# A two-block transformer kernel on one Trainium2 core: a new order of the steps where one stage hands x to the next

## The reference

```python
for l in range(2):
    h = rms_norm(x, g[0]); x = x + 0.5 * rms_norm(swiglu(h, w1[l,0], w3[l,0], w2[l,0]), g[1])
    h = rms_norm(x, g[2]); x = x + rms_norm(mixer_block(h, w_in[l], ...), g[3])
    h = rms_norm(x, g[4]); x = x + rms_norm(cross_attention(h, rms_norm(mem), ...), g[5])
    h = rms_norm(x, g[6]); x = x + 0.5 * rms_norm(swiglu(h, w1[l,1], w3[l,1], w2[l,1]), g[7])
```

## Time and profile before

| | us |
|---|---|
| runs of the kernel before: lowest, median, highest | 2435.52, 2442.23, 2451.49 |
| the profiled execution, whole | 2452.16 |
| its span, from first to last instruction | 2450.3 |
| TensorE busy in the span | 2280.1 |
| VectorE busy | 1712.3 |
| ScalarE busy | 1182.3 |
| mean granted TensorE clock, share of full speed | 0.956 |

### The profile page before, as it was taken

One profiled execution on the slowest core, in us unless ns is written; L12 is line 12 of the kernel. 1 busy time (PEld: TensorE's weight loads), 2 busy tenths in 40 slices (PEclk: granted clock), 3 DMA queues, 4 the chain that ended last, 5 costly groups with the idle time before them and its releaser, 6 DMA issues.

```text
span 2450.3 us, 43494 instructions
## 1 busy us (share of the span) xinstructions
PE 2280.1 (93%) x17809; PEld 2178.7 (89%) x17809; DVE 1712.3 (70%) x2733; ACT 1182.3 (48%) x1843; POOL 91.6 (4%) x86
## 2 busy tenths in 40 slices
PE   6998898999999999989898998999899989797998
PEld 5977798999999897889797998999897889797998
DVE  6666887986665797777555665665797787555664
ACT  2564446764544434455434454444434454534443
POOL 1000000110110000000000110010000000000010
PEclk7998999999999999899999999999899899899999
DMA  8634585667657463346443765666553345453664
GB/s 238 194 106 144 161 257 156 201 190 225 190 177 222 138 181 91 108 142 194 128 157 114 203 185 162 184 195 194 161 178 94 104 146 182 128 173 96 198 184 134
DMA packets 399909, 405.08 MB, mean 165 GB/s; under 512 B 18182, under 2 KB 392312, under 8 KB 399713
## 3 DMA queue, kind: packets, MB, share of 16 engines
q1 hardware_dynamic: 396177, 389.27, 52.5%
q0 software_dynamic: 3536, 13.04, 1.7%
HBM read 401.17 MB, written 1.09 MB: 164 GB/s over the span
## 4 chain that ended last, share of the span: by engine, by line
PE 72%; DVE 18%; ACT 6%; issue 4%; DMA 1%; DVEq 0%; ACTq 0%; POOL 0%; POOLq 0%
PE gemm_ps L934 46%; PE gemm_ps L937 15%; DVE weights_lo L1557 6%; DVE x_res L2023 4%; PE misc_ps L1075 2%; PE misc_ps L1076 2%; ACT weights_hi L1191 1%; DVE mod_partial L1656 1%; ACT e L1358 1%; PE misc_ps L872 1%; PE misc_ps L1108 1%; ACT squares L1315 1%; PE misc_ps L1093 1%; PE misc_ps L1072 1%; DVE y L1731 1%
## 5 line engine op out<-in xcount | busy, mean ns | idle before, releaser
L1557 DVE TENSOR_TENSOR weights_lo<-raw_weights,weights_hi 128x1024 fp32r<-128x1024 f32 x704 | 836.8, 1199 | 430.4 <-ACT weights_hi L1191 426.9
L1191 ACT CAST weights_hi<-raw_weights 128x1024 fp32r<-128x1024 f32 x704 | 717.6, 1032 | 658.9 <-PE gemm_ps L934 457.1
L934 PE MATMUL gemm_ps<-h_hi,weights_hi 128*128 128x256 f32 x3280 | 939.0, 286 | 20.0 <-DVE h_lo L1685 8.7
L934 PE MATMUL gemm_ps<-h_lo,weights_hi 128*128 128x256 f32 x3280 | 922.1, 281 | 0.0
L934 PE MATMUL gemm_ps<-h_hi,weights_lo 128*128 128x256 f32 x3280 | 921.5, 281 | 0.0
L934 PEld LDWEIGHTS gemm_ps<-h_hi,weights_hi 128*128 128x128 f32 x3280 | 631.5, 193 | 27.7 <-issue 21.0
L934 PEld LDWEIGHTS gemm_ps<-h_lo,weights_hi 128*128 128x128 f32 x3280 | 630.9, 192 | 3.4 <-issue 3.0
L934 PEld LDWEIGHTS gemm_ps<-h_hi,weights_lo 128*128 128x128 f32 x3280 | 630.1, 192 | 0.0
L2023 DVE SCALAR_TENSOR_TENSOR x_res<-zp,param_cols,x_res 128x256 f32<-128x256 f32 x480 | 196.7, 478 | 0.0
L937 PE MATMUL gemm_ps<-weights_hi,hidh 128*128 128x256 f32 x688 | 189.9, 276 | 0.0
L937 PE MATMUL gemm_ps<-weights_hi,hidl 128*128 128x256 f32 x688 | 189.9, 276 | 0.0
(11 more groups left out here) (324 smaller groups left out, 3144.9 us busy)
## 6 DMA issues: line engine op xcount, KB each, us to landing
raw_weights<-in_ffn_w_dram SPq DMA_DIRECT2D x256, 512.0 KB, 4.2
raw_weights<-in_w_in_dram SPq DMA_DIRECT2D x200, 512.0 KB, 3.8
raw_weights<-in_w_mod_dram SPq DMA_DIRECT2D x48, 512.0 KB, 5.0
raw_weights<-in_w_up_dram SPq DMA_DIRECT2D x44, 512.0 KB, 4.6
raw_weights<-in_xattn_kv_dram SPq DMA_DIRECT2D x32, 512.0 KB, 3.7
raw_weights<-in_w_out_dram SPq DMA_DIRECT2D x24, 512.0 KB, 4.1
raw_weights<-in_w_down_dram SPq DMA_DIRECT2D x20, 512.0 KB, 4.7
raw_weights<-in_w_branch_dram SPq DMA_DIRECT2D x16, 512.0 KB, 4.6
```

What stands on the lines that cost most here:

```text
L934: mm = pe.matmul(ps[:, c, 0:T], w[:, m, kt, c * P:(c + 1) * P], x[:, f, :], start=start, stop=stop_)
L1191: act.copy(unit_of(WH, m % SPLIT, u), unit_of(RAWB, u["raw"] % RAW, u)).then_inc(sems["weights_rounded"], 1)
L1557: dve.tensor_tensor(unit_of(WL, m % SPLIT, u), unit_of(RAWB, u["raw"] % RAW, u), unit_of(WH, m % SPLIT, u), ALU.subtract).then_inc(sems["w ...
```

## The change

All of it is at the seven changes of stage.

1. **Late conversion.** For the last unit m of a stage's last product (c = 3; `w2` and `xattn_o`, not `w_out_2`), `hi(m+3)` is issued behind `y_rstd`'s two instructions on ScalarE, and `lo(m+3)` on VectorE just ahead of `row_wide`, which stands behind all updates and splits. The seven changes have three of `w2`, two of `xattn_o` and two of `w_out_2`.
2. **Ten matmuls** (`warm`) on the constant tiles ones and ident, fp32, 128x128 by 128x128, into PSUM bank 2, behind the stage's last work on TensorE and ahead of the first turn. Nothing reads what they write.
3. **Turning.** Tiles 0 to 3 are all turned ahead of the first unit, into four banks (f % 4); a turn waits for the split of tile f-4. Tiles 4 and 5 are turned ahead of k-tiles 2 and 3 of the first unit, 6 and 7 ahead of k-tiles 0 and 1 of the second. The order on VectorE stays.
4. **The row.** VectorE's wide copy becomes a step of its own (`row_wide`) inside `enter`, ahead of `lo(m+4)` and `lo(m+5)` in VectorE's queue. The step `x_row` (TensorE's two matmuls, ScalarE's copy) goes behind the first unit of the second gemm.

```diff
     def gemm(...):
             u["turn_h"] = turns_of_h.pop(j, None)
+            u["late"] = j == n - 1 and k.get("c") == 3 and w != "w_out_2"
             units.append(u)
             readers[x[0]] = u["n"]
             add("unit", **u)
+            S.extend(row_next)
+            row_next.clear()
         S.extend(held)
         held.clear()
+        row_next.extend(row_due)
+        row_due.clear()
         add(evac, **p)
...
     def enter(key, name, at_):
+        s = new_stat()
         k = dict(key=key, v=xv[0])
         h = dict(buf="H", gen=key, src="turned", ...)
+        add("warm", n=10)
         add("update_x", p=0, **res)
-        for f in (0, 1):
-            add("turn_h", f=f, **k)
+        add("update_x", p=1, **res)
+        for f in range(4):
+            add("turn_h", f=f, s=s if f == 3 else None, **k)
         for p in range(4):
-            if p == 0:
-                add("update_x", p=1, **res)
-            elif p > 1:
+            if p > 1:
                 add("update_x", p=p, **res)
             for f in (2 * p, 2 * p + 1):
                 add("split", f=f, **h)
-        for j in range(2):
-            turns_of_h[j] = [dict(k, f=f) if f < NF else None for f in range(4 * j + 2, 4 * j + 6)]
-        s = new_stat()
+        turns_of_h[0] = [None, None, dict(k, f=4), dict(k, f=5)]
+        turns_of_h[1] = [dict(k, f=6), dict(k, f=7), None, None]
         add("x_rstd_tok", key=key, v=xv[0])
-        held.append(("x_row", dict(key=key, s=s)))
+        add("row_wide", key=key)
+        row_due.append(("x_row", dict(key=key, s=s)))
...
         def pe_turned(k):
-            if f >= 3:
-                pe.wait_ge(sems["vec_split"], at("split", "H", k["key"], f - 3))
+            if f >= 4:
+                pe.wait_ge(sems["vec_split"], at("split", "H", k["key"], f - 4))
+        def pe_warm(k):
+            ...
+            for i in range(k["n"]):
+                pe.matmul(TURN[:, 0:P], ONES[:], IDENT[:], start=True, stop=True)
         def pe_turn_h(k):
+            if k["f"] == 3:
+                stat_free(k["s"])
...
     # ScalarE's walk of the list
             if kind == "unit":
-                hi(k["m"] + AHEAD)
+                if k["late"]:
+                    state["late"] = k["m"] + AHEAD
+                else:
+                    hi(k["m"] + AHEAD)
             if kind in parts:
                 parts[kind](k)
+            if kind == "y_rstd" and state["late"] is not None:
+                hi(state["late"])
+                state["late"] = None
...
     # VectorE's walk of the list
+            if kind == "row_wide" and state["late"] is not None:
+                lo(state["late"])
+                state["late"] = None
             if kind == "unit":
-                lo(k["m"] + AHEAD)
+                if k["late"]:
+                    state["late"] = k["m"] + AHEAD
+                else:
+                    lo(k["m"] + AHEAD)
```

More of the change, by code:

```diff
@@ L96, in plan @@
     turns_of_h = {}
+    row_due, row_next = [], []
     def add(kind, **k):
@@ L755, in source @@
         if k["src"] == "turned":
-            return PB[:, k["f"] % 3, 0:T]
+            return PB[:, k["f"] % 4, 0:T]
         return BUF[k["src"]][:, k["f"], :]
@@ L868, in pe_turned @@
             pe.wait_ge(sems["vec_norm"], at("x", k["v"], f // 2))
-            if f >= 3:
-                pe.wait_ge(sems["vec_split"], at("split", "H", k["key"], f - 3))
+            if f >= 4:
+                pe.wait_ge(sems["vec_split"], at("split", "H", k["key"], f - 4))
             for t in range(TT):
-                mm = pe.transpose(PB[:, f % 3, t * P:(t + 1) * P], XT[:, t, f * P:(f + 1) * P], IDENT[:])
+                mm = pe.transpose(PB[:, f % 4, t * P:(t + 1) * P], XT[:, t, f * P:(f + 1) * P], IDENT[:])
             mm.then_inc(sems["pe_norm"], 1)
             up("pe_norm", ("h_turned", k["key"], f))
+        def pe_warm(k):
+            if state["att"] is not None:
+                pe.wait_ge(sems["vec_attn"], at("o_raw", *state["att"]))
+                if state["att"][0][:4] == "diff":
+                    pe.wait_ge(sems["act_attn"], at("o_sq", *state["att"]))
+            for i in range(k["n"]):
+                pe.matmul(TURN[:, 0:P], ONES[:], IDENT[:], start=True, stop=True)
         def pe_turn_h(k):
@@ L1170, in pe_mem_turn @@
                 up("pe_norm", ("mem_ps", k["l"], half))
-        parts = dict(unit=pe_unit, window=pe_window, params=pe_params, turn_x=pe_turn_x, mod=pe_mod, mod_col=pe_mod_col, bias=pe_bias, stat=pe_stat, x_stat=pe_x_stat, turn_h=pe_turn_h, x_tok=pe_x_tok, x_row=pe_x_row,
+        parts = dict(unit=pe_unit, warm=pe_warm, window=pe_window, params=pe_params, turn_x=pe_turn_x, mod=pe_mod, mod_col=pe_mod_col, bias=pe_bias, stat=pe_stat, x_stat=pe_x_stat, turn_h=pe_turn_h, x_tok=pe_x_tok, x_row=pe_x_row,
                      rstd_cols=pe_rstd_cols, qk_norm=pe_qk_norm, scores=pe_scores, turn=pe_turn, pv=pe_pv,
@@ L1182, in _ @@
     def _(act):
-        state = dict(rq=None, y_sum=None)
+        state = dict(rq=None, y_sum=None, late=None)
         def hi(m):
@@ L1542, in _ @@
             if kind == "unit":
-                hi(k["m"] + AHEAD)
+                if k["late"]:
+                    state["late"] = k["m"] + AHEAD
+                else:
+                    hi(k["m"] + AHEAD)
             if kind in parts:
                 parts[kind](k)
+            if kind == "y_rstd" and state["late"] is not None:
+                hi(state["late"])
+                state["late"] = None
     @block.vector
     def _(dve):
+        state = dict(late=None)
         gain_of = {k["key"]: GAIN[k["tile"]] for kind, k in steps if kind == "gain"}
@@ L1733, in vec_update_x, with vec_row_wide @@
                 up("vec_norm", ("x", k["v"], p))
-        def vec_x_row(k):
+        def vec_row_wide(k):
             dve.wait_ge(sems["act_norm"], at("rstd_tok", k["key"]))
@@ L2074, in _ @@
         parts = dict(setup=vec_setup, params=vec_params, turn_x=vec_turn_x, mod=vec_mod, mod_sum=vec_mod_sum, adapt=vec_adapt, split=vec_split,
-                     residual=vec_residual, evac_ytok=vec_ytok, update_x=vec_update_x, x_row=vec_x_row, rstd_cols=vec_rstd_cols, evac_qk=vec_evac_qk, qk_norm=vec_qk_norm,
+                     residual=vec_residual, evac_ytok=vec_ytok, update_x=vec_update_x, row_wide=vec_row_wide, rstd_cols=vec_rstd_cols, evac_qk=vec_evac_qk, qk_norm=vec_qk_norm,
                      evac_scaled=vec_scaled, evac_v2=vec_v2, softmax=vec_softmax, pv=vec_pv, subln=vec_subln,
```

## The result

The changed kernel took 2378.2 us (median of 4 runs, 2374.4 to 2382.1) against 2443.8 for the kernel before (4 runs, 2435.5 to 2451.5): ratio 0.9732, 95% interval 0.9696 to 0.9769. It is 65.6 us faster. The forecast was 2380. The profiled execution took 2374.4 us, 77.8 less than the profiled one of before.

A forecast was written before the change was run, and what follows sets the result against it. TensorE was busy for 93% of the span, so only its waits and lower-clock work could be won. Terms 2.2 + 17.0 + 48 - 5 = 62 us gave 2390 from the profiled 2452.2, 2380 against the median 2442.2; range 2364 to 2411.

The forecast's parts named there:

- the clock's term: At the stage changes, one further low-clock stretch of 3.4 us in three of seven: -5 us, bounds 0 and -12.
- first update sooner: At three changes behind a `w2`, late conversion lets the first update of x start 0.74 us sooner: 2.2 us.
- turns and two units: From first update through turns and first two units, seven changes: 76.6 us against 93.6, a gain of 17.0.
- the row: wait, its matmuls, clock, less the late remainder: At the row, seven changes: 33.4 us wait, 2.9 for its matmuls, 14 of lower clock, less 2.2: gain 48.
- the late remainder: `lo(m+3)`, ending 0.43 us after TensorE could start the third unit, at five changes: 2.2 us lost.
- The chain worked out for the first change: Step-by-step times of updates, turns, splits and first two units after the first update's start U, ending at U + 10.95.
- the forecast's own range: The whole kernel's time: 2366 to 2394 us, from the clock's two bounds and 7 us for the chain; chance 0.62.
- the last gap of 1.5 us: TensorE's wait for update 3, U + 6.26 to 7.75, before turns 6 and 7; the clock could fall or not.
- The rival of the falling clock: The clock falls at the changes all the same: 29 us lost in place of 5, gain 38, 2404; chance 0.22.
- The weights' rival: The row's wait turns into waits for `lo` weights: 21 us lost, gain 41, 2401; chance 0.12.
- the dry ring: Rival: raw buffers freed 12 us later starve TensorE of loads, 17 us slower, 2459; chance 0.03.
- The ten's own price: Ten matmuls at each stage change take 0.22 us each, 2.2 in all, inside TensorE's wait, so cost nothing.

The follow-up runs named there:

- old turns: The changed kernel with the old order of the turns (three banks, two tiles turned first): ratio 0.9736 to the kernel before, against 0.9705 for the changed kernel.
- ten alone: The kernel before with only the ten matmuls added, in front of the first update of x: 2440.2 us, ratio 0.9968 to the kernel before.
- row alone: The changed kernel with ten matmuls, late conversion and new turning undone, leaving the row's move: 2397.1 us, ratio 0.9786 to the kernel before.
- all but the row: The changed kernel with the row put back where it was, wide copy and TensorE's part: 2435.9 us, ratio 0.9938 to the kernel before.

## Why the prediction was right, point by point

The time came out 2 us from the forecast, and the terms can be told apart in the traces. That it is so close is partly luck: two terms came out 1 and 2 us short and the clock's term 5 us too low, and a ratio of the same kernel moved by 0.003 (7 us) between two measurements.

| term | forecast, us | measured in the traces | runs that bear on it |
|---|---|---|---|
| first update sooner (three changes) | 2.2 | 2.2 | without the late conversion: 2.0 between the medians, inside their spread |
| turns and two units | 17.0 | 15.3 | old turns 8, ten alone 8 |
| the row: wait, its matmuls, clock, less the late remainder | 48 | 47 | row alone 52, all but the row 15 |
| a low stretch at three of seven changes | -5 | 0 | none in any trace with the ten in place and the row's copy moved |
| sum | 62 | 64 | 65.6 between the medians |

- *First update.* 1.65 us behind the last matmul was read from the third change; 1.66 was measured at the first. I had booked the same 2.2 us as lost at the third unit, so that the late conversion came out at nothing. That was wrong: the trace without it has the fourth unit waiting instead, so the wait for the late remainder takes nothing from the ninth unit on.
- *Turns and units.* From the first turn to the end of the second unit: 71.1 us over seven changes for 86.4 before, by the same reading. The chain worked out for the first change was met within 0.3 us at each of its points; its end, U + 10.95, was measured at U + 11.16.
- *How that term splits* is where my step failed in part. I had put the whole of it under the new order of the turns. By the traces 8.8 us came with the ten matmuls in the old order, the full clock's part (86.4 to 77.6), and 6.5 us with the new order (77.6 to 71.1).
- *The row.* The mechanism and its price were right. The runs add that two thirds of the wait (22.5 of 33.4) hung on the copy's place on VectorE and one third on TensorE's unit; in time, with the clock, 39 us and 9.5. (In the working, 2.1 us seven times is 14.7 and not 14, and the lower end of the forecast's own range should be 2368 and not 2366; neither matters.)
- *The clock.* The -5 was mis-sized. I took the last gap of 1.5 us for a coin toss; the trace has 1.22 us there, and the clock fell at none of 14 changes in two profiled runs of the changed kernel. With gaps of 0.2 to 1.2 us, and of 1.6 at the row in one version, the granted clock stayed at 1.00. The Trainium skill ("TensorE: Matmul & The Clock Gate", section "A second HAM failure mode: psum-queue depth-cycling") has a kernel whose frequent small idle spells between groups of matmuls made the clock swing. These changes don't show that.
- *The rival of the falling clock* was priced at 4.2 us a change, by a chain with every matmul at half speed. In the versions without the ten the clock did fall, at four or five changes of seven, but for 3.4 us only, and for part of those TensorE was waiting on VectorE anyway. It cost 3 us in all, not 29. The weights' rival and the dry ring did not occur: 5.9 us of waits for `lo`, and no wait for a load behind the kernel's start.
- *The ten's own price.* 0.22 us each by the row; the ten took 2.39 us with the last one's tail, which is again 0.22 each; ten more took 2.23 us more (4.62). The Trainium skill ("TensorE: Matmul & The Clock Gate", section "Back-to-back issue gap") has 134 cycles for 128 columns in a table that names no type; the estimate from it was 0.56 us for the ten. The row was the better guide by a factor of four.

## What to carry to other kernels

A wait of the busiest engine is first a question of what stands ahead of its releaser in that engine's queue: here one 0.3 us copy stood behind two conversions of which nothing was due yet, and moving it ahead of them and its consumer one unit back was worth 52 of 66 us. Filling an idle stretch with useless matmuls does keep the clock up, but what that is worth depends on who sets the pace in the stretch behind it, and on how often the clock would have fallen: here 0.8 us for each fall and 3 us in all where the other engines set the pace, 1.25 and 9 once TensorE was busy for nearly all of the stretch. So mend the order first and fill last, and never beyond the idle time. Price a low clock only on those matmuls of the low stretch that nothing else holds up.

## What the runs showed that I had not expected

The same unchanged code ran with very different amounts of low clock from one execution to the next. Around the second block's first attention part, windows of the kernel before:

```profile
970.00:988.00 18.00, 15.39 (x55) 12.17 (x56) 13.02 (x30) 6.33 (x13) 0.00 (x0) 0.53 0.28 89
997.00:1005.00 8.00, 8.00 (x34) 6.74 (x34) 8.00 (x15) 1.55 (x2) 0.00 (x0) 0.57 0.45 131
```

The changed kernel, whose same part lies some 12 us earlier in its span:

```profile
958.00:973.00 15.00, 12.37 (x42) 9.15 (x43) 12.24 (x28) 4.59 (x9) 0.00 (x0) 0.54 0.33 103
```

And the version with twenty matmuls:

```profile
965.00:970.00 5.00, 4.18 (x18) 3.64 (x18) 5.00 (x12) 2.32 (x5) 0.00 (x0) 0.66 0.35 105
970.00:1005.00 35.00, 34.11 (x232) 28.78 (x232) 30.08 (x63) 19.77 (x40) 0.00 (x0) 1.00 0.35 106
```

That is 17.1 us at the lower clock and a further 6.8 in the first, 13.6 in the second, and 3.4 in the third, after which it was full for 35 us. Nothing in these versions differs there but when the stretch begins. The parts outside the changes of stage had 132 us at the lower clock in the profiled execution of before and 117 in that of the changed kernel. The two profiled executions differ by 77.8 us, 14 beyond the 64 of the changes. A stretch at half the clock costs at most half its length, so the difference of 15 us at the lower clock can account for at most 7 of these 14; that it does was not tried, and the rest stays open. The executions of one kernel spread over 8 to 25 us, so a change of a few us at one place has to be read from the trace of that place: the time alone could not show the ten matmuls' 3.3 us in five runs.
